# Moving three products on TensorE in a three-block decoder kernel: a value product, an output strip's bank order, and the last routing scores

## What is computed

```python
def stick_breaking_attention(q, k, v):            # 16 heads of 64, 256 tokens
    z = einsum(q_blk, kt) * scale
    mask = kpos[None, :] < qpos[:, None]
    log_keep = where(mask, log_sigmoid(-z), 0.0)
    log_survive = cumsum(log_keep, reverse=True) - log_keep
    weights = where(mask, exp(log_sigmoid(z) + log_survive), 0.0)
    return einsum(weights, vt)                    # then @ odd_w_out

def peer(h, w_query, sub_keys1, sub_keys2, expert_u, expert_v):
    q = (hf @ w_query)                            # 16 chunks of 128 columns
    s1, s2 = q[:, :, 0] . sub_keys1, q[:, :, 1] . sub_keys2
    v1, i1 = top_k(s1, 16); v2, i2 = top_k(s2, 16)
    vc, ic = top_k(v1 + v2, 16)                   # routing
    a = gelu(hf @ expert_u.T) * gate              # here for all 16384 experts
    return a @ expert_v
```

## Time and profile before

| | |
|---|---|
| median of 3 runs | 1543.62 us (1543.27 to 1550.52) |
| the profiled execution, its own time | 1543.07 us |
| its span in the trace | 1541.1 us |
| PE busy | 1517.0 us, 98% |
| DVE busy | 1239.4 us, 80% |
| ACT busy | 866.9 us, 56% |
| waits of PE, the sum of the view's 17 rows | 19.8 us |
| POOL busy | 229.2 us, 15% |
| share of PE in the chain that ended last | 81%, DVE 14% |

### The profile page before, as it was taken

The page is one execution under the profiler, slowest core; times in us unless marked ns, Lnnn a source line. Parts: engine busy times, 40 slices in busy tenths (PEclk is TensorE's granted clock), DMA queues, the critical chain, the costliest instruction groups (busy, mean ns, idle before and its releaser), DMA issues.

```text
span 1541.1 us, 30293 instructions
## 1 busy us (share of the span) xinstructions
PE 1517.0 (98%) x10109; PEld 1315.2 (85%) x10109; DVE 1239.4 (80%) x2363; ACT 866.9 (56%) x1393; POOL 229.2 (15%) x99
## 2 busy tenths in 40 slices
PE   8899999999999999999999999999999999999999
PEld 8788888889888888998988888888888888888887
DVE  8978888755788887775899986999999999965555
ACT  7964444568744446675666566555555444444453
POOL 1010000125100001000678746100000000000000
PEclk9999999999999999999999999999999999999999
DMA  6155555543465655434455556555554555555554
GB/s 232 43 158 176 186 191 191 176 152 123 151 215 184 192 191 175 150 123 164 151 166 190 173 183 201 178 168 173 169 172 164 177 170 172 175 180 193 194 195 151
DMA packets 72493, 264.56 MB, mean 172 GB/s; under 512 B 8048, under 2 KB 8304, under 8 KB 72048
## 3 DMA queue, kind: packets, MB, share of 16 engines
q1 hardware_dynamic: 71712, 260.97, 52.2%
q10 hardware_dynamic: 720, 2.77, 0.5%
HBM read 262.66 MB, written 1.05 MB: 171 GB/s over the span
## 4 chain that ended last, share of the span: by engine, by line
PE 81%; DVE 14%; ACT 2%; issue 2%; DMA 1%; POOL 0%; DVEq 0%; ACTq 0%; SPq 0%
PE ps L753 34%; PE ps L609 20%; PE ps L613 11%; DVE arena L1910 4%; PE ps L1263 2%; PE ps L577 2%; PE ps L581 2%; PE ps L578 2%; PE ps L667 1%; DVE arena L2584 1%; DVE arena L2585 1%; DVE arena L2587 1%; DVE arena L2586 1%; DVE arena L2583 1%; DVE w_lo L1910 1%
## 5 line engine op out<-in xcount | busy, mean ns | idle before, releaser
L1354 ACT ACTIVATE w_hi<-ring 128x1024 fp32r<-128x1024 f32 x489 | 515.1, 1057 | 369.0 <-PE ps L753 206.8
L1910 DVE TENSOR_TENSOR w_lo<-ring,w_hi 128x1024 fp32r<-128x1024 f32 x397 | 483.9, 1221 | 56.0 <-ACT w_hi L1354 50.2
L609 PE MATMUL ps<-hT,w_hi 128*128 128x512 f32 x1696 | 427.1, 394 | 1.9 <-DVE arena L1910 0.9
L609 PEld LDWEIGHTS ps<-hT,w_hi 128*128 128x128 f32 x1696 | 307.1, 189 | 59.5 <-DVE arena L1910 1.6
L2830 POOL TENSOR_TENSOR w_lo<-ring,w_hi 128x1024 fp32r<-128x1024 f32 x92 | 224.1, 2443 | 742.0 <-DVE w_lo L1910 390.9
L753 PE MATMUL ps<-w_hi,halves_hi 128*128 128x512 f32 x688 | 271.9, 395 | 0.6 <-DVE halves_lo L1910 0.4
L753 PE MATMUL ps<-w_hi,halves_lo 128*128 128x512 f32 x688 | 268.8, 391 | 0.0
L613 PEld LDWEIGHTS ps<-hT,w_lo 128*128 128x128 f32 x1696 | 231.1, 190 | 17.4 <-DVE w_lo L1910 0.7
L613 PE MATMUL ps<-hT,w_lo 128*128 128x256 f32 x1696 | 236.6, 282 | 0.0
L753 PE MATMUL ps<-w_lo,halves_hi 128*128 128x512 f32 x688 | 185.4, 390 | 0.0
L753 PEld LDWEIGHTS ps<-w_lo,halves_hi 128*128 128x128 f32 x688 | 129.0, 188 | 28.0 <-DVE w_lo L1910 0.6
(11 more groups left out here) (360 smaller groups left out, 1808.5 us busy)
## 6 DMA issues: line engine op xcount, KB each, us to landing
ring<-in_strips SPq DMA_DIRECT2D x489, 512.0 KB, 3.5
const<-in_const SPq DMA_DIRECT2D x1, 1384.0 KB, 11.6
x_s<-in_x SPq DMA_DIRECT2D x2, 512.0 KB, 4.5
arena<-in_rel ACTq DMA_DIRECT2D x1, 1024.0 KB, 4.7
arena<-in_keys ACTq DMA_DIRECT2D x1, 1024.0 KB, 6.1
out<-x_s SPq DMA_DIRECT2D x4, 256.0 KB, 2.2
arena<-in_ssm_bc SPq DMA_DIRECT2D x1, 512.0 KB, 8.0
arena<-in_ssm_b SPq DMA_DIRECT2D x1, 512.0 KB, 8.8
```

The costliest lines, as they stand in the source:

```text
L609: pe.matmul(bank, w[0][:, c * P:(c + 1) * P], hT[:, c].rearrange("p s t -> p (s t)"), start=c == 0, stop=False, skip_group_check=True)
L1354: sc.activation(w_hi[:, n % RING, :], ring[:, n % RING, :], ACT.Copy).then_inc(high_ready, 1)
L1910: return ve.tensor_tensor(o, a, b, op)
```

## The change

Three edits, and one that goes with the third.

1. In `odd` on PE, before: q(2), k(2), ov(0), z(2), cum(1), q(3), k(3), ov(1), z(3), cum(2). After: q(2), k(2), z(2), q(3), ov(0), cum(1), k(3), ov(1), z(3), cum(2). From pair 4 on nothing changes.
2. The first output strip of `odd` works token block 1 (banks 2 and 3) before block 0, in its high-half products. Block 1 waits for `w_masked` 6, block 0 for 7, in place of one wait for 7 before both.
3. In `peer`, key_scores(15) stands behind up(0), and up(0) waits for all projections but the last to be out. On ACT a call that makes high halves stands ahead of key_copy(15) in place of behind it. The banks of the up strips are swapped (5, 4, 2 for 4, 5, 2).

```diff
@@ up_bank
-            return (4, 5, 2)[e % 3] if e < HALF else 5 - e % 2
+            return (5, 4, 2)[e % 3] if e < HALF else 4 + e % 2
@@ rows
-            def rows(w, hi, lo, first, last, turn=None):
+            def rows(w, hi, lo, first, last, turn=None, masked=None):
...
-                    for a in range(NT):
+                    for a in range(NT) if masked is None else (1, 0):
+                        if masked is not None:
+                            pe.wait_ge(w_masked, masked - a)
@@ out_rows
-                         n == 0, n == KC - 1, 2 * i + 1 if n == KC - 1 else None)
+                         n == 0, n == KC - 1, 2 * i + 1 if n == KC - 1 else None, 7 if name == "odd" and n == 0 else None)
@@ odd, on PE
-                for j in range(2, 8):
+                for n in range(2):
+                    proj_fm(("odd", "qk"[n], 2))
+                z(2)
+                proj_fm(("odd", "q", 3))
+                ov(0)
+                cum(1)
+                proj_fm(("odd", "k", 3))
+                ov(1)
+                z(3)
+                cum(2)
+                for j in range(4, 8):
                     proj_fm(("odd", "q", j))
                     proj_fm(("odd", "k", j))
                     ov(j - 2)
                     z(j)
                     cum(j - 1)
-                pe.wait_ge(w_masked, 7)
                 out_rows(1, "odd", range(2))
@@ peer, on PE
                 key_scores(2 * PH - 2)
-                key_scores(2 * PH - 1)
-                pe.wait_ge(evac, nproj[0])
+                pe.wait_ge(evac, nproj[0] - 1)
...
                     strip_wide(ps[:, up_bank(e), :], w, 6 if e == 0 and i is None else None)
+                    if e == 0 and i is None:
+                        key_scores(2 * PH - 1)
@@ peer, on ACT
                 key_copy(2 * PH - 2)
+                base = AT[("peer", "u", 0)]
+
+                high_to(base + RING - 2)
                 key_copy(2 * PH - 1)
-                base = AT[("peer", "u", 0)]
-
-                high_to(base + RING - 2)
```

More of the change, by code:

```diff
@@ L1806, in peer @@
                 key_copy(2 * PH - 2)
-                key_copy(2 * PH - 1)
                 base = AT[("peer", "u", 0)]
                 high_to(base + RING - 2)
+                key_copy(2 * PH - 1)
                 ch.add(sc.activation(stat[:, 7:8], k("eps"), ACT.Gelu))
```

## The result

The kernel with all three edits takes 1550.81 us (median of 16 runs, 1548.16 to 1556.91) against 1543.31 us before (16 runs, 1542.95 to 1550.63). The ratio is 1.0042, with a 95% interval of 1.0029 to 1.0055, so the change made the kernel slower by about half a per cent, where 1544.7 was forecast. Most kernels here, the one before too, have a part of their executions some 7 us above the rest (3 of the 16 after, 4 of the 16 before), which count in every median, range and ratio, so that a ratio also moves with how many of them each side happened to have.

The account below looks back on a forecast made before the run. PE, busy in 98% of the span, was taken to bound the kernel. Terms +2.0 - 0.95 + 0.1 = +1.15 us on 1543.07 gave 1544.2, or 1544.7 as median; range 1540.5 to 1548.5.

Parts of the forecast that it names:

- Edit 1: +2.0 us: Moving ov(0) and cum(1) behind q(3) in pairs 2 and 3 costs 2.0 us; bounds -1.45 and +2.3.
- z(2) needs project(2): z(2) waits for DVE's project(2) copy, ending 345.24, so it starts at 345.29 after PE stands 2.14 us.
- DVE's list then makes softplus(2) late: On DVE softplus(2) queues behind ov_copy(0) and weights(1), starting at 352.25 instead of 350.27: 1.98 us lost.
- nothing repeats from pair 4 on: Edit 1's loss does not recur in z(3) to z(7); the rival that it repeats, 1554.7, had chance 0.02.
- The step from softplus(2) at 352.25 to z(3) later by 1.98: project(3) stands behind softplus(2) on DVE, so z(3) moves from 354.26 to 356.24 and PE idles 1.4 us.
- TensorE's clock falls in the longer stall: Rival: 1.2 GHz after edit 1's 2.14 us stall, each projection strip 2.95 us longer, total slower beyond 0.5%; chance 0.01.
- the trace gives it no support: Dismissal of the skill's clock-gate rule: granted clock read 1.00 around the 1.45 us stall and behind the 7.3 us one.
- Edit 2: First output strip: half its eight products, 0.97 us, fit before 393.04; forecast -0.95 us, bounds 0 and 1.05 gain.
- Edit 3: Moving key_scores(15) behind up(0) removes a 1.58 us wait, but DVE's up_add takes it back; forecast +0.1 us.
- The waits of up(2): up(2) waits for late high and low halves, so of 1.58 us some 0.5 is left when up(3) starts.
- the wait at 882.56: PE's 0.69 us wait for DVE's up_add in the up strips grows by 0.5, leaving 0 gain at 888.
- forecast as 1.4: PE's idle time before z(3) in pair 3 under edit 1: 1.4 us.

Follow-up runs that it names:

- e1_dve: Edit 1 on the kernel before, POOL's q(4) low half delayed, unused products in first stall, softplus(2)'s first two operations earlier on DVE: 1544.44 us, ratio 1.0004.
- e1_both: Edit 1 on the kernel before, POOL's q(4) low half delayed, 9 and 5 unused PE products in the two stalls: 1545.61 us, ratio 1.0014.
- e1_filler: Edit 1 on the kernel before, with 9 and 14 unused PE products in the stalls before z(2) and z(3): 1547.70 us, ratio 1.0021.
- e1_fill1: Edit 1 on the kernel before, with 9 unused PE products in the first stall only: 1554.23 us from six runs, ratio 1.0061.
- e1_only: Edit 1 alone on the kernel before: 1551.43 us against 1543.34, ratio 1.005.
- e3_only: Edit 3 alone on the kernel before, with the order on ACT left as before: 1543.13 us, ratio 0.9999.
- e23: Edits 2 and 3 without edit 1 on the kernel before, ACT's order left as before: 1542.46 us against 1543.29, ratio 0.9991.
- the mended versions: All three edits with what `e1_both` or `e1_dve` adds to edit 1: 1545.01 us (ratio 0.9996) and 1544.24 us (ratio 1.0004).

## Why the prediction was wrong

**The sum of edit 1.** The step that failed is "Edit 1: +2.0 us" with its bounds of -1.45 and +2.3. The profiles divide the real cost, since all that lies behind z(3) is the same work:

| | z(3) starts | from there to the end | span |
|---|---|---|---|
| before | 354.26 | 1186.8 | 1541.1 |
| `e1_dve` | 355.46 | 1186.9 | 1542.4 |
| `e1_both` | 356.63 | 1186.8 | 1543.4 |
| `e1_filler` | 358.73 | 1186.8 | 1545.5 |
| `e1_fill1` | 358.62 | 1188.4 | 1547.0 |
| `e1_only` | 359.94 | 1188.5 | 1548.4 |

The order on DVE, with the wait for q(3)'s low half in it, costs 356.63 - 354.26 = 2.4, the hold beside POOL 358.73 - 356.63 = 2.1, the clock behind the first stall 359.94 - 358.73 = 1.2, and the clock behind the second 1188.5 - 1186.8 = 1.7, which `e1_fill1` shows by itself as 1.6. The clock behind the first takes 1.7 from PE by the windows too, but some 0.5 of it falls on the time that q(3) would wait for its low half at full speed. Each term is good to some 0.2 us: z(2), ahead of which the five with edit 1 differ in nothing but fillers, starts between 345.15 and 345.37.

The four terms come to 7.3 us by these executions, and edit 1 costs 8.1 by the medians; the profiled `e1_only` reads 0.998 as granted clock over the whole execution, and five others of its twelve, at 1550.97 to 1551.55, read 0.997, which points to one more fall in them. By the medians the order costs 2.3, the hold 2.1 (`e1_filler` less `e1_both`) and the clock 3.7 (`e1_only` less `e1_filler`).

- *Right in it:* z(2) needs project(2), starts at 345.35 (345.29 forecast) after 2.14 us; DVE's list then makes softplus(2) late; the size, 2.0 (bound 2.3) against 2.3 to 2.4; and nothing repeats from pair 4 on, since what follows z(3) takes as long as before.
- *Missing:* DVE's operations moved against POOL's, and each was costed at its length from another pair. The step from softplus(2) at 352.25 to z(3) later by 1.98 assumed that what lies between keeps its length. It ran into POOL's low half of q(4), which starts when ACT's high half is there: ACT's Exp of weights(1) had moved too, and the high half is queued behind it. In the kernel before, POOL's low half began 0.84 us behind the same operation of DVE:

```profile
352.58 0.96 DVE L1910 TENSOR_TENSOR halves_lo<-arena,halves_hi 128x768 fp32r<-128x768 f32 x1
...
353.42 4.73 POOL L2830 TENSOR_TENSOR w_lo<-ring,w_hi 128x1024 fp32r<-128x1024 f32 x2 [2.70 <-ACT w_hi L1354]
```

After, DVE's stood 3.6 us later and POOL's 2.4, so POOL's came first, by 0.32 (355.86 and 356.18). The slow clock moved both alike: with the clock up, in `e1_filler`, it is 2.4 and 1.2 us, and POOL's is first by the same 0.32 (354.63 and 354.95). The margin was less than the 1.2 us by which DVE's moved more than POOL's, and no row that the prediction read showed it.
- *The two multiply:* without the hold the second stall is 1.23 us, and the clock stays at 1.00 behind it in the execution shown; with it the stall is 3.26 and the clock fell in every profile that has it (with no filler in it).

**The rival that came.** "TensorE's clock falls in the longer stall" was given 0.01 and cost 2.9 us by the executions and 3.7 by the medians, the largest part. The evidence against it was thin: the earlier trace rows show that the clock survives a stall of 1.45 us, which is shorter than both of the new ones, and its state in the kernel's first microseconds, which is not a stall in steady work. Neither covers a longer stall. It was also priced as a rival by itself, which needed 2.3 strips at half clock, each 2.95 longer, to pass 7.7 us; a fall took 1.7 us from PE, little more than half of one such strip, and was one term of three. The rule that the prediction cited (the Trainium skill, "TensorE: Matmul & The Clock Gate", part 1: the clock is throttled by default and activity releases it) agrees with the 0.50 behind both stalls, and "the trace gives it no support" was said of stalls too short to tell.

**Edit 2** was forecast at -0.95. Medians and spans give -1.2, of which 0.4 stands ahead of the edit in the profiled execution, so some -0.8 is its own. The mechanism is as described: half a strip fits in front of weights(6).

**Edit 3** was forecast at +0.1 and measured at -0.2 by the medians and 0.0 by the spans. The waits of up(2) came as 0.39 and 0.37, and 0.57 of the gain was left behind them, where 0.5 was forecast. That DVE's up_add takes it back is right, the place isn't: it went at 811.79, in a wait that the kernel before doesn't have, and the wait at 882.56, which was to grow by 0.5, stayed at 0.70.

**What the three make.** 8.1 - 1.2 - 0.2 = 6.7 us, against 7.5 by the medians of after and before. The profiled execution after is 4.1 us slower than that behind z(3) (1551.7 - 359.89 = 1191.8, against 1188.5 - 0.8 = 1187.7). The lines of DVE from 785 to 895 us show where (out<-in, count | busy, mean ns): its pair sums, two inputs from SBUF, first after, then in the kernel with edit 3 alone:

```profile
L1922 DVE TENSOR_TENSOR arena<-arena 128x256 f32<-128x256 f32 x13 | 20.5, 1580 | 0.1
```

```profile
L1911 DVE TENSOR_TENSOR arena<-arena 128x256 f32<-128x256 f32 x13 | 16.2, 1243 | 0.1
```

4.3 us more for the same 13 operations, each of which lasts from 0.42 (free) to 2.7 us (begun beside a low half of POOL). up_add is queued behind them, PE waits 1.92 us at 837, and the clock falls once more. Neither `e3_only` nor `e23` nor the mended versions show it (16.2 in each), and after's median is 2.9 below this execution. Why the two engines met so badly in this execution stays open; it was not tried apart. It isn't quite alone: one other of the sixteen, at 1553.39, is as slow, and five more, at 1550.27 to 1550.99, read a granted clock of 0.996 or 0.997, where those at 1549.17 to 1549.67, which are the sum of edit 1's profile and edit 2's gain (1550.37 - 0.8 = 1549.6), read 0.998. So falls beyond the two of edit 1 come in about half of the executions after; where they lie is seen in one only.

## What to carry to other kernels

When an instruction is moved, write out anew the list of every engine that waits on it, and look at what each shifted operation will then stand beside: here a stall of 1.23 us, forecast as 1.4, grew to 3.26 because a DVE operation slid into one of POOL's. A stall of 2 us on TensorE in steady work is to be priced with its clock (here up to 1.7 us more for each), and a trace with shorter stalls only is no evidence against it. An engine that paces a stretch (DVE's up_add from 811.79 on) takes back what another gains ahead of it, so the gain of a removed wait is worth nothing until that pacer is found.

## What the runs showed of the hardware

- **A DVE operation with two inputs from SBUF waits for a POOL operation that has begun.** 128x768: 0.96 us alone, 2.98 to 3.02 beside POOL; 128x512: 0.68, then 2.88; 128x256: 0.42, then up to 2.7. The end is POOL's end plus the operation's own length, to 0.13 us (330.27 + 2.40 + 0.68 = 333.35 against 333.22 in the kernel before; 359.22 against 359.17 after). It goes the other way too: POOL's two low halves at 355.86 take 5.51 us where two take 4.73 in `e1_both`. An operation with one input from PSUM is not held: up_add (arena<-ps,xn, 128x256) takes 0.42 us on the mean among POOL's low halves. The Trainium skill ("SBUF — State Buffer", section "SBUF: two separate sides") has this as a rule, an exclusive lock between the two engines for a VectorE instruction with two SBUF inputs, held for the whole instruction; these numbers agree with it.
- **The granted clock after a stall in the middle of work.** Behind the waits of 1.05 to 1.77 us it stayed at 1.00 in the kernel before (the 1.77 is at 70.56 us, before L913, in a stretch of small products). Behind the one wait of 1.92 us it fell (0.66 in 836 to 841), behind 2.14 us it was 0.50 in two profiles and 1.00 in one, and behind 3.26 to 3.31 us 0.50 in all three. Each fall behind the two stalls of edit 1 lasted some 3 us and cost 1.2 to 1.7.
- **Useless products pay.** Nine in one stall and fourteen in the other, 5.7 us of PE's time, made the kernel 3.7 us faster by the medians than edit 1 alone, and 2.8 by the profiled executions.
